# A two-block transformer kernel: modulation columns, output weights and recurrence products placed elsewhere

## What is computed

```python
def first_block(x, ...):
    h = rms_norm(x, norm_w);  z = h @ w_in        # split in 9
    # attention in 3 groups (window 128, 512, 2048; dilation 1, 4, 16), merged by their softmax sums
    y_a = (merged * silu(g_a)) @ w_proj_a
    # gated linear recurrence, 8 heads of 128, chunks of 32 tokens, forwards and backwards
    y_b = (rms_norm(o_fwd + o_bwd, hg_norm_w) * silu(g_b)) @ w_proj_b
    return x + (sigmoid(zgate_a) * y_a + sigmoid(zgate_b) * y_b) @ w_out

def step(state, xs):                              # one chunk of the recurrence
    q_n, k_n, v_n, dec_n = xs
    o_n = einsum('bhik,bhkv->bhiv', q_n, state)
    state = dec_n[..., None] * state + einsum('bhik,bhiv->bhkv', k_n, v_n)
    return state, o_n

def second_block(x, c, ctx, c_ctx, ...):
    for i in range(2):                            # ctx: 256 further tokens
        sh1, sc1, g1, sh2, sc2, g2 = split(silu(c) @ ada_w[i] + ada_b[i], 6)     # the context has its own six
        h = rms_norm(x, norm1_g[i]) * (1 + sc1) + sh1
        y = even_mixer(h, hc) if i == 0 else odd_mixer(h, hc)
        x = x + g1 * y
        h = rms_norm(x, norm2_g[i]) * (1 + sc2) + sh2
        x = x + g2 * expert_choice_ffn(h, ...)    # 16 experts, each takes its best tokens
        # the context rows go the same way, in layer 0 alone
```

## Time and profile before

| what | value |
|---|---|
| median of three runs | 4846.86 us |
| the profiled execution | 4835.65 us, its span 4833.9 us |
| mean granted clock of TensorE | 0.88 of full |
| busy share of TensorE, VectorE, ScalarE, GpSimd | 80, 29, 15, 2% |
| DMA, whole span | 627 MB, mean 130 GB/s |
| DMA in the busiest fortieths of the span, experts' stages | 362 to 403 GB/s |

### The profile page before, as it was taken

The page is one execution under the profiler, slowest core; times in us unless marked ns, Lnnn a source line. Parts: engine busy times, 40 slices in busy tenths (PEclk is TensorE's granted clock), DMA queues, the critical chain, the costliest instruction groups (busy, mean ns, idle before and its releaser), DMA issues. The chain is left out here.

```text
span 4833.9 us, 55527 instructions
## 1 busy us (share of the span) xinstructions
PE 3880.0 (80%) x23423; PEld 2353.0 (49%) x23423; DVE 1380.8 (29%) x2575; ACT 720.9 (15%) x1357; POOL 114.5 (2%) x88
## 2 busy tenths in 40 slices
PE   7997698989977875984799976887878678847776
PEld 4666266565533542853333324577777535522222
DVE  2313222213321077533100002245554324320000
ACT  1112001001011023311100001122222212110000
POOL 0000000000000000000111110000000000000000
PEclk9988799888889987996899998977888889969999
DMA  3100122332451100013799982000000100159999
GB/s 113 70 18 2 57 99 86 126 122 96 134 186 55 36 21 0 1 44 123 278 396 397 394 294 82 22 1 1 2 2 2 63 30 10 54 205 403 403 402 362
DMA packets 237723, 627.40 MB, mean 130 GB/s; under 512 B 39284, under 2 KB 87396, under 8 KB 230438
## 3 DMA queue, kind: packets, MB, share of 16 engines
q1 hardware_dynamic: 227430, 600.78, 33.2%
q0 software_dynamic: 10048, 23.07, 2.1%
HBM read 589.07 MB, written 34.75 MB: 129 GB/s over the span
## 5 line engine op out<-in xcount | busy, mean ns | idle before, releaser
L377 PE MATMUL bank<-weights_l,hT_l 128*128 128x512 f32 (+2 forms) x1824 | 607.9, 496 | 40.7 <-DMA weights_l<-in_w_in 20.5
L377 PEld LDWEIGHTS bank<-weights_l,hT_l 128*128 128x128 f32 x1824 | 388.1, 217 | 258.9 <-issue 176.7
L373 PE MATMUL bank<-hT_l,weights_l 128*128 128x512 f32 (+1 forms) x928 | 329.2, 518 | 39.2 <-DMA weights_l<-in_w_in 24.6
L1721 PE MATMUL bank<-expert_weights_l,expert_tokensT_l 128*32 128x512 f32 x3072 | 338.8, 597 | 11.0 <-DMA expert_weights_l<-in_moe_w 9.6
L1921 PE MATMUL bank<-expert_weights_l,expert_tokensT_l 128*64 128x512 f32 x1024 | 246.4, 629 | 86.2 <-DMA expert_weights_l<-in_moe_w 85.1
L373 PEld LDWEIGHTS bank<-hT_l,weights_l 128*128 128x128 f32 x928 | 179.0, 194 | 188.0 <-issue 164.5
L1234 PE MATMUL bank<-hT_l,gate_weights_r 128*128 128x512 f32 x384 | 223.3, 735 | 18.5 <-DMA gate_weights_r<-in_w_in 18.5
L1721 PEld LDWEIGHTS bank<-expert_weights_l,expert_tokensT_l 128*32 128x32 f32 x3072 | 107.4, 110 | 228.3 <-issue 221.8
L1921 PEld LDWEIGHTS bank<-expert_weights_l,expert_tokensT_l 128*64 128x64 f32 x1024 | 80.9, 143 | 241.4 <-issue 182.6
L1756 PE MATMUL bank<-expert_weights_l,rows 128*32 128x512 f32 x1536 | 167.9, 592 | 0.9 <-ACT rows L1796 0.9
L377 PE MATMUL bank<-weights_l,mixedT_l 128*128 128x512 f32 x320 | 142.0, 607 | 27.8 <-DMA weights_l<-in_ev_w_out 14.9
(11 more groups left out here) (472 smaller groups left out, 5237.2 us busy)
## 6 DMA issues: line engine op xcount, KB each, us to landing
expert_weights_l<-in_moe_w SPq DMA_DIRECT2D x192, 2048.0 KB, 25.1
ada_weights_r<-in_ada_w SPq DMA_DIRECT2D x48, 1024.0 KB, 5.0
weights_l<-in_w_in SPq DMA_DIRECT2D x10, 2048.0 KB, 7.9
weights_l<-in_w_in SPq DMA_DIRECT2D x16, 1024.0 KB, 5.3
gate_weights_r<-in_w_in SPq DMA_DIRECT2D x12, 1024.0 KB, 6.3
weights_l<-in_od_w_in SPq DMA_DIRECT2D x7, 1024.0 KB, 5.4
gate<-gate_rows_r SPq DMA_DIRECT2D x24, 256.0 KB, 2.4
weights_l<-in_ev_w_in SPq DMA_DIRECT2D x3, 2048.0 KB, 10.8
```

Source lines behind the costliest of these rows:

```text
L373: ins = pe.matmul(bank[:n, :m], w_sb[:, k, s:s + n], xT[:, k, t:t + m], start=k == 0, stop=k == kt - 1)
L377: ins = pe.matmul(bank[:rows_of_tile(x), :n], x, w_sb[:, k, :n], start=k == 0, stop=k == kt - 1)
L1721: return pe.matmul(bank[q * STRIP:(q + 1) * STRIP, :], xs[:, k, e, g * STRIP:(g + 1) * STRIP], w[:, j, h * HALF:(h + 1) * HALF], start=k = ...
```

## The change

- `products` puts each bank's product and its eviction in the queues one after the other, and after each calls `between` if there is one; `dense` hands it through.
- In the recurrence `kv(i, n)` multiplies keys by values for two chunks at once, head by head in turns between them, into both banks; it stands before `inter(i)` of every even `i` and waits for state `i`, where `kv(i + 1)` waited for one state less. A pass has seven such pairs, 28 in all, and one single `kv` at its end.
- `modulation_columns` makes the columns of both layers and all four scales, once, in `branches_merged` between the `w_proj_b` and the `w_out` product; they stay in SBUF.
- `gated_output` gets its gate rows and first weights from `output()`, a context opened before `attend` in both mixers. In the even layer the gate rows take the place of `um`, the latent input, and the weights a new ring of 256 columns; in the odd layer the ring of 512 is used.
- `rwkv_outputs` yields before every single product (`by_pair`), the square is VectorE's, and one yield stands behind the root instead of before it. `inputs` is no generator any more: one step of `rwkv_outputs` is taken after each bank of the three projections, and these banks are emptied by ScalarE alone. What is left of the steps follows.
- In the odd layer the second norm runs inside `neighbourhood`, after its loads and memsets.

```diff
         if g0 + i >= nb:
             pe.wait_ge(*core.emptied_by[g0 + i - nb])
-        fill(pe, i, core.bank[(g0 + i) % nb]).then_inc(core.filled.sem, core.filled.one())
-    for i in range(n):
+        bank = core.bank[(g0 + i) % nb]
+        fill(pe, i, bank).then_inc(core.filled.sem, core.filled.one())
         if who(i) == "v":
             dve.wait_ge(core.filled.sem, f0 + i + 1)
-            take(dve, i, core.bank[(g0 + i) % nb]).then_inc(core.emptied_v.sem, core.emptied_v.one())
-    for i in range(n):
-        if who(i) == "s":
+            take(dve, i, bank).then_inc(core.emptied_v.sem, core.emptied_v.one())
+        else:
             act.wait_ge(core.filled.sem, f0 + i + 1)
-            take(act, i, core.bank[(g0 + i) % nb]).then_inc(core.emptied_s.sem, core.emptied_s.one())
+            take(act, i, bank).then_inc(core.emptied_s.sem, core.emptied_s.one())
+        if between:
+            between()
...
-                        def kv(i):
-                            c = order[i]
-                            r = slice((c % 4) * CH, (c % 4) * CH + CH)
+                        def kv(i, n):
                             if i >= 2:
-                                pe.wait_ge(state_done.sem, at[0] + i - 1)
+                                pe.wait_ge(state_done.sem, at[0] + i)
                             for hh in range(HB):
-                                ins = pe.matmul(kv_bank[i % 2][:, hh * P:hh * P + P], ks[r, c // 4, hh * P:hh * P + P],
-                                                v[r, c // 4, hc + hh * P:hc + hh * P + P], start=True, stop=True)
-                            ins.then_inc(kv_filled.sem, kv_filled.one())
+                                for j in range(i, i + n):
+                                    c = order[j]
+                                    r = slice((c % 4) * CH, (c % 4) * CH + CH)
+                                    ins = pe.matmul(kv_bank[j % 2][:, hh * P:hh * P + P],
+                                                    ks[r, c // 4, hh * P:hh * P + P],
...
                         core.settle(dve)
                         update(0)
                         for i in range(1, NCH):
-                            if i + 1 < NCH - 1:
-                                kv(i + 1)
+                            if i % 2 == 0:
+                                kv(i, min(2, NCH - 1 - i))
                             inter(i)
                             if i < NCH - 1:
                                 update(i)
...
         dense(core, oT, HH, SEQ, I["w_proj_b"], 0, D, take, transposed=True, who=lambda i: "v", early=early)
+        modulation_columns(core, I, C, mod_dram)
...
-def modulation_columns(core, C, mod_dram, layer, cols):
+def modulation_columns(core, I, C, mod_dram):
+    dve, step = core.nc.vector, core.step
+    cols, scales = C["cols"], C["scales"]
     with core.scope() as sb:
-        rows = sb("mod_rows", [2 * 6 * KT, P])
-        core.load(rows[:, :], mod_dram[layer].rearrange("w (j p) -> (w j) p", p=P))
-        transposes(core, [(cols, [rows[:, :]])], C["ident"])
-def norm_scales(core, cols, norm_g, layer, sc, scale):
-    dve = core.nc.vector
-    step, landed, stored = core.step, core.landed, core.stored
-    with core.scope() as sb:
-        g = sb("norm_gain", [P, KT])
-        load_columns(core, g[:, :], norm_g, layer * D, KT)
+        rows = sb("mod_rows", [2 * 6 * KT, 2, P])
+        g = sb("norm_gains", [P, 2, 2, KT])
+        for layer in range(2):
+            core.load(rows[:, layer, :], mod_dram[layer].rearrange("w (j p) -> (w j) p", p=P))
+            for j, name in enumerate(("norm1_g_2", "norm2_g_2")):
+                load_columns(core, g[:, layer, j, :], I[name], layer * D, KT)
+        transposes(core, [(cols[:, layer].rearrange("p w j k -> p (w j k)"), [rows[:, layer, :]]) for layer in range(2)],
+                   C["ident"])
         core.settle(dve)
-        dve.tensor_scalar(scale, cols[:, :, sc, :], 1.0, None, ALU.add).then_inc(step.sem, step.one())
-        dve.wait_ge(step.sem, step.n)
-        dve.tensor_tensor(scale, scale, mid(g[:, :], 2), ALU.mult).then_inc(step.sem, step.one())
+        for layer in range(2):
+            for j, sc in enumerate((SC1, SC2)):
+                linked(dve, core.link_v, dve.tensor_scalar(scales[:, layer, j], cols[:, layer, :, sc, :], 1.0, None, ALU.add))
+                dve.tensor_tensor(scales[:, layer, j], scales[:, layer, j], mid(g[:, layer, j, :], 2), ALU.mult) \
+                    .then_inc(step.sem, step.one())
```

```diff
-def gated_output(core, catT, w, X, mod_dram, layer, tokens, ss):
+def gate_rows(core, mod_dram, layer, g):
+    for which in range(g.shape[1]):
+        load_rows(core, g[:, which, :], mod_dram, (layer * 2 + which) * MOD + G1 * D, D)
+def gated_output(core, catT, w, X, mod_dram, layer, tokens, ss, g, early):
     dve, act = core.nc.vector, core.nc.scalar
     step, link = core.step, core.link_v
...
         core.settle(act)
-        dense(core, catT, KT, tokens, w, 0, D, take, who=lambda i: "v", ready=False)
+        dense(core, catT, KT, tokens, w, 0, D, take, who=lambda i: "v", ready=False, early=early)
         for t in range(nt):
-            act.wait_ge(core.emptied_v.sem, base + (D // BANK - 1) * nt + t + 1)
+            act.wait_ge(core.emptied_v.sem, base + (D // core.ring[0].shape[2] - 1) * nt + t + 1)
...
         ring += [sb("expert_weights", [P, DEEP, D]) for _ in range(SLOTS - AHEAD)]
         if nx > NT:
             experts_in_strips(core, I, C, X, layer, mod_dram, sel_dram, xs, sums, ring, sem)
         yield from headed(1)
```

```diff
                       lambda e, tt, col, n, ps: copy(core, e, um[:, tt, col:col + n], ps), ready=False, early=early)
                 conformer_inputs(core, I, C, hT, padded[:, :, :], taps[:, :, :], norm[:, :, :])
+        rows = um[:, 0:4, :].rearrange("p t n -> p (t n)")[:, 0:2 * D].rearrange("p (w n) -> p w n", w=2)
+        w = I["ev_w_out_2"][0]
+        @contextmanager
+        def output():
+            with core.weight_ring(256):
+                gate_rows(core, mod_dram, 0, rows)
+                early = prefetch(core, KT, w, 0, D)
+                yield
+                gated_output(core, catT, w, X, mod_dram, 0, ALLTOK, ss, rows, early)
         latent_attention(core, I, C, um, catT[:, 0:4, :],
-                         lambda other: conformer(other, C, padded, taps, norm, catT[:, 4:8, :]))
```

```diff
+        def by_pair(fill, take):
+            for c in range(RCT):
+                yield True
+                products(core, 1, lambda pe, i, bank: fill(pe, c, bank), lambda e, i, bank: take(e, c, bank))
         yield True
         total(Y, 0.0)
-        yield True
-        products(core, RCT, spread, lambda e, c, bank: e.tensor_tensor(Y[:, c, :], Y[:, c, :], bank[:, :], ALU.subtract))
-        core.settle(act)
-        act.activation(sq[:, :, :], Y, ACT.Square).then_inc(step.sem, step.one())
...
         core.settle(act)
         act.activation(stat[:, :], stat[:, :], ACT.Sqrt).then_inc(step.sem, step.one())
+        yield True
         dve.wait_ge(step.sem, step.n)
         dve.reciprocal(stat[:, :], stat[:, :]).then_inc(step.sem, step.one())
-        yield True
-        products(core, RCT, spread, lambda e, c, bank: e.scalar_tensor_tensor(
+        yield from by_pair(spread, lambda e, c, bank: e.scalar_tensor_tensor(
             out=Y[:, c, :], in0=Y[:, c, :], scalar=col[:, COL_GG, c:c + 1], in1=bank[:, :], op0=ALU.mult, op1=ALU.mult))
-        yield True
-        products(core, RCT, lambda pe, c, bank: pe.matmul(bank[:, :], g2[:, c * P:c * P + P], gate[:, :],
-                                                          start=True, stop=True),
-                 lambda e, c, bank: e.scalar_tensor_tensor(
-                     out=Y[:, c, :], in0=Y[:, c, :], scalar=col[:, COL_GB, c:c + 1], in1=bank[:, :],
-                     op0=ALU.add, op1=ALU.mult))
-def neighbourhood(core, I, C, hT, outT, early, beside_inputs):
+        yield from by_pair(
+            lambda pe, c, bank: pe.matmul(bank[:, :], g2[:, c * P:c * P + P], gate[:, :], start=True, stop=True),
+            lambda e, c, bank: e.scalar_tensor_tensor(out=Y[:, c, :], in0=Y[:, c, :], scalar=col[:, COL_GB, c:c + 1],
+                                                      in1=bank[:, :], op0=ALU.add, op1=ALU.mult))
```

```diff
         load_bias(0)
         load_bias(1)
-        def inputs():
+        normed(hT, True)
+        def inputs(between):
+            by_scalar = lambda i: "s"
             w, c0 = I["od_w_in_2"][0], RW_IN
             with core.scope() as sb2:
                 x = [sb2("q", [P, NT, W]), sb2("k", [P, NX, W])]
                 def project(j):
                     dense(core, hT, KT, x[j].shape[1] * P, w, c0 + j * W, W,
-                          lambda e, tt, col, n, ps: copy(core, e, x[j][:, tt, :], ps), ready=j > 0, early=early[j:j + 1])
+                          lambda e, tt, col, n, ps: copy(core, e, x[j][:, tt, :], ps), who=by_scalar, ready=j > 0,
```

(25 more changed lines are left out.)

152 lines of the change are left out of this document (70 added, 82 removed).

## The result

The changed kernel takes 4763.11 us, the median of four runs (4756.62 to 4766.97), against 4847.51 us for the kernel before in the same comparison. The ratio is 0.9832 (95% interval 0.9818 to 0.9847): 84.4 us less. On another chip it came out at 0.9842 (0.9824 to 0.9861). The forecast was 4760.

A forecast was written before the change was run, and what follows sets the result against it. No engine bounds all stages: between them all wait in `settle`, and the last runs on weight transfers. Terms -18.7 + 12.4 - 25.3 - 29.0 - 20.6 = -81.2 us gave 4754.4 or 4765.7, forecast 4760, range 4722 to 4798.

The forecast's parts named there:

- Recurrence: Key-value products of two chunks in turns: 0.85 us net for each of 22 pairs, 18.7 us less.
- I leave that as it is: Recurrence's gate products: the low clock after small products was counted as unchanged; staying at 2.4 GHz could save up to 45 us.
- the second rival: Recurrence: clock stays up, half to all gate blocks start at 2.4 GHz, 22 to 45 us more saved; chance 0.14.
- the 1.93 of the forecast: Recurrence: bound for a pair of chunks' products without overlap, 1.93 us, against 1.08 expected.
- The rule of the Trainium skill that was held against the change: Recurrence, under rival 1: tiling speeds products, not what empties the bank; it would give that rival's time, 4779 us.
- Columns before `w_out`: Before the `w_out` product: six small loads delay its weights, 12.4 us more, bounds 8 and 15.
- Norms: Columns made once save 7.1 us (even layer), 11.0 (two feed-forwards), 5.5 and 1.7 (odd layer's norms): 25.3 less.
- the window will land about 3861: Odd layer's second norm: window lands behind 4 MB of weights issued at 3845.76; TensorE starts at 3890.2, 1.7 us less.
- Outputs between banks: Odd projections: waits lose 17.8 us, spread products 6.3, dense products 5.3: 29 us less, bounds 10 and 31.
- the dense products fall towards 117.0: Odd projections: 272 dense products go from 124.9 towards 117.0 us, 5.3 less after excepting 2.6 for their first start.
- Output weights: Output products in both layers: shorter pauses less new gate-row waits, net 20.6 us less, 10.7 even and 9.9 odd.
- the turns give nothing: Recurrence, rival 1: two-strip products overlap less or the update becomes the bound; 4779 us, chance 0.15.
- the pieces wait: Odd projections, rival 3: VectorE's queue holds pieces up and TensorE idles, 10 us saved instead of 29; 4779 us, chance 0.13.

The follow-up runs named there:

- e1: Changed kernel with the key-value products placed as before, one chunk at a time: 4791.67 us, ratio 0.9906.
- e2: Changed kernel with the pairs kept in place but their products issued chunk by chunk, not in turns: 4763.08 us, ratio 0.9842.
- g3: Changed kernel with columns' loads early, gate rows on their own semaphore, odd second norm's small loads before weights, and pairs chunk by chunk: 4719.67 us, ratio 0.9761.
- f5: Changed kernel with the first two `w_out` loads requested ahead of the six loads of modulation rows and gains: 4753.45 us, ratio 0.9833.
- f6: Changed kernel with modulation and gain loads requested at the branches' start on their own semaphore, `w_out` weights ahead of the transposes: 4741.38 us, ratio 0.9806.
- f8: Changed kernel with gains, window and bias requested before the odd second norm's 4 MB of weights, memsets during the rows' reload: 4738.17 us, ratio 0.9797.
- e4: Changed kernel with gate rows and first output weights requested after attention, as before, in both layers: 4769.74 us, ratio 0.9861.

## Why the forecast came out

The time was right within 3 us, and most terms were too. But the recurrence gave 15 us more than forecast and the other terms together some 12 less, so a good part of the nearness is luck.

**Recurrence: -18.7 forecast, -33.6 measured.** What the forecast priced came out: the pair at 1.09 us for 1.08, key-value products 32.2 less for 28 x 1.08 = 30.2, a wait of 5.9 more for 6.4, and 5.5 hidden by waits for gate weights for 5.1. That makes 20.8 for 18.7. What the forecast had wrong is "I leave that as it is", said of the clock. The clock rose in this stage from 0.85 to 0.88, 25 blocks of gate products were short instead of 17, and the gate products gave 9.6. The products with the state gave 4.6, which the forecast did not price; how much of that is the clock was not separated. The rise comes with the pairs and not with the turns: 17 short blocks at 0.85 with single chunks (e1), 23 and 24 at 0.87 with pairs out of turn (e2, g3). It is the second rival at less than half of its least price, 9.6 of 22 and 8 blocks instead of 14, so by its words it did not occur.

On the overlap the sizes were right, though the row behind them was read wrongly. The 0.107 us a product came from two chunks that stand together, 1.71 us, and these overlap already, as in e2; 1.98 for a pair without overlap, near the 1.93 of the forecast, follows from single groups. What the forecast missed is that most of the gain does not need the turns: chunk by chunk a pair takes 1.64, the products with the state gain by standing together (72.6 to 65.6 us), the clock rises too, and the waits fall. The stage gains 28 us so, or 31 against e1; the turns add 2 to 7.

The rule of the Trainium skill that was held against the change (TensorEngine Tiling (Array Packing), PSUM Bottleneck: tiling speeds up the products and not what empties the bank) describes what the turns ran into: with them the state's update by VectorE is what the second product waits for, 16.4 us against 8.4. It did not decide the change, because most of the gain comes without the turns.

**Columns before `w_out`: +12.4 forecast, +11.7 measured;** f5 shows that the loads' place in the queue is not the price, and f6 that it goes when they are requested early.

**Norms.** Even layer -6.2 (7.1 forecast), first feed-forward -7.8 less 1.8 of the product = -6.0 (5.5), odd layer's first -4.6 (5.5), last feed-forward -7.1 less 1.9 = -5.2 (5.5). Second norm of the odd layer: +0.5 for -1.7. The step "the window will land about 3861" had the window 15.2 us behind the weights' issue; it was 16.9. (The terms of that step add up to 3889.8 and not to 3890.2.) The mechanism, a wait behind the weights in place of the modulation's, agrees with f8, where it goes, together with the memsets.

**Outputs between banks: -29 forecast,** -21.8 in the stage and 4.0 of waiting for gate rows inside it: -25.8. The 17.8 of waits went whole. The spreads fell by 4.3 instead of 6.3, and "the dense products fall towards 117.0" was the term that failed: 122.0 (from 124.9), although the clock is at 0.98 there. A bank of a projection takes 7.07 us from its first matmul to the spread behind it (3885.94 to 3893.01), 0.442 for each of its 16, at the full clock, where the clean stretch of the earlier trace rows has 0.430. Why it is slower was not settled.

**Output weights: -20.6 forecast,** measured +7.1 - 15.2 - 1.8 in the even layer and +4.0 - 10.7 - 1.9 in the odd one: -18.5. The waits for gate rows were 6.36 and 3.92 for the 6.05 and 4 of the forecast. What the forecast did not see is that about half of the even gain comes from the narrower ring (5.0 us by e4).

**Not forecast:** +3.3 us behind the last router. The clock of the stretch with the transposes and router products was 0.59 instead of 0.70 and the stretch lasted 19.9 for 16.7 us. With the output weights late (e4) the stage was 54.1 us again, and 57.1 to 57.8 in every other changed kernel; so it hangs on the early request, but how the clock comes to rise later there was not settled.

The sum of the terms was -81.2 and the medians give -84.4: 15 too little in the recurrence, against some 12 too much in the others. The range, 4722 to 4798, held it. The rivals "the turns give nothing" and "the pieces wait" were both refuted as forecasts of the time; the first was nearly true of the turns alone.

## What to carry to other kernels

When a change both groups small products and interleaves them, price the grouping by itself: pairs in plain order gave here some 28 to 31 us, part of it by an overlap that the order has anyway, and the turns 2 to 7 more, since the next engine's update took back half of what they saved. Before an experiment is taken for one "without overlap", count in its trace what is in flight. A load moved to another place is free only if it is requested before the engines stand still, and if nothing between waits on a semaphore that counts all loads: three waits of this kind (11.7, 10.4 and 17.2 us) held back almost half as much again as the change brought. Ask of every stretch that a change shortens what the clock may do behind it: here it gave 9.6 us that nobody had counted. Compare profiles stage by stage, and ask of a stage that nobody touched how much it moves by itself before a difference of 10 us is given a cause.

## What was not expected of the hardware

- The state recurrence, with the same 7840 matmuls, took 779 to 800 us in thirteen profiled executions, at granted clocks of 0.85 to 0.82. Between two profiled executions of one kernel (4764.7 and 4749.2 us) it makes 6.6 of the 15.5 us; the stage before the first key-value product makes 6.4 and the recurrence 3.4.
- Sixteen products of 32 rows took 1.64 us chunk by chunk and 1.09 in turns between two strips, where two groups of eight with another kind between them took 2.16. Chunk by chunk the second strip began behind the fifth product of the first and ran beside its last three.
- Halving the first chunk of weights, 2 MB to 1 MB, cut a pause that waited for it from 14.89 to 9.94 us.
